# Products of zeros on TensorE in the first stage, and the 32 lag transfers issued by SyncE and GpSimd only

## What is computed

```python
hn = rmsnorm(x, even_norm)
q, k, v, u = split(hn @ even_w_in)             # 256 x (512, 128, 128, 512)
# state-space mixer, for each of 32 groups g of 16 channels, 64 complex states:
dt = exp(log_dt); lam = exp(a * dt)            # a complex, one per state
bb = (lam - 1) / a * b                         # input matrix
h_t = lam * h_(t-1) + bb @ u_t                 # scan over the 256 tokens
y_t = real(c @ h_t) + d_skip * u_t
y = gelu(y); o_ssm = y * sigmoid(y @ w_glu + b_glu)
o_attn = swa_sink_attention(rmsnorm(q), rmsnorm(k), v, sinks)
x = x + concat(o_attn, o_ssm) @ even_w_out
```

## Time and profile before

| | |
|---|---|
| median of 3 runs | 1210.29 us (1207.67 to 1211.19) |
| the profiled execution, its own time | 1210.32 us |
| its span in the trace | 1208.6 us, so 1.7 us lie around it |
| PE busy | 98% |
| PEld, DVE, ACT, POOL busy | 85%, 65%, 49%, 6% |
| mean granted clock of TensorE | 0.997 of full speed |
| chain that ended last | PE 92%, DVE 3%, ACT 2%, DMA 1%, SPq 1% |

### The profile page before, as it was taken

One profiled execution on the slowest core, in us unless ns is written; L12 is line 12 of the kernel. 1 busy time (PEld: TensorE's weight loads), 2 busy tenths in 40 slices (PEclk: granted clock), 3 DMA queues, 4 the chain that ended last, 5 costly groups with the idle time before them and its releaser, 6 DMA issues.

```text
span 1208.6 us, 17835 instructions
## 1 busy us (share of the span) xinstructions
PE 1185.3 (98%) x7139; PEld 1026.1 (85%) x7139; DVE 783.1 (65%) x848; ACT 588.8 (49%) x730; POOL 67.1 (6%) x87
## 2 busy tenths in 40 slices
PE   6999999999999999999999999999999999999997
PEld 5876888888999988888888888888889988888886
DVE  6956676666755557666667666667594646766665
ACT  4547643434566645434345444445574545443443
POOL 2120000000002110000000000000011000000000
PEclk9999999999999999999999999999999999999999
DMA  7254565656544355656555556565543534656561
GB/s 196 92 145 141 162 207 177 200 179 202 180 140 168 113 168 181 207 177 196 185 191 168 199 178 205 177 204 175 175 133 116 183 127 134 197 185 197 179 202 70
DMA packets 156104, 205.81 MB, mean 170 GB/s; under 512 B 7752, under 2 KB 129168, under 8 KB 156048
## 3 DMA queue, kind: packets, MB, share of 16 engines
q1 hardware_dynamic: 154944, 203.30, 52.2%
q10 hardware_dynamic: 944, 1.52, 0.6%
q0 software_dynamic: 160, 0.20, 0.1%
HBM read 202.77 MB, written 1.05 MB: 169 GB/s over the span
## 4 chain that ended last, share of the span: by engine, by line
PE 92%; DVE 3%; ACT 2%; DMA 1%; SPq 1%; issue 0%; POOL 0%; POOLq 0%; ACTq 0%
PE outp L754 26%; PE outp L695 20%; PE acc L695 20%; PE outp L758 14%; PE acc L806 3%; PE outp L713 1%; DMA raw<-in_even_w_in_dram 1%; PE outp L1193 1%; DVE w_lo L2198 1%; PE outp L725 1%; DVE h_pair L2243 1%; PE outp L860 1%; SPq L517 1%; PE acc L1173 1%; ACT w_hi L1650 0%; ACT h_pair L1711 0%
## 5 line engine op out<-in xcount | busy, mean ns | idle before, releaser
L1650 ACT ACTIVATE w_hi<-raw 128x2048 fp32r<-128x2048 f32 x177 | 339.4, 1918 | 413.0 <-PE outp L758 283.2
L2198 DVE TENSOR_TENSOR w_lo<-raw,w_hi 128x2048 fp32r<-128x2048 f32 x177 | 405.3, 2290 | 177.0 <-ACT w_hi L1650 176.9
L754 PE MATMUL outp<-h_pair,w_hi 128*128 128x512 f32 x1056 | 253.9, 391 | 0.3
L754 PEld LDWEIGHTS outp<-h_pair,w_hi 128*128 128x128 f32 x1056 | 195.0, 188 | 42.7 <-DVE h_pair L2243 4.2
L758 PEld LDWEIGHTS outp<-h_pair,w_lo 128*128 128x128 f32 x1056 | 135.4, 191 | 5.2
L695 PE MATMUL acc<-w_hi,f_lo 128*128 128x512 f32 x352 | 137.4, 390 | 0.0
L695 PE MATMUL acc<-w_hi,f_hi 128*128 128x512 f32 x352 | 137.4, 390 | 0.0
L695 PE MATMUL acc<-w_lo,f_hi 128*128 128x512 f32 x352 | 137.1, 389 | 0.0
L758 PE MATMUL outp<-h_pair,w_lo 128*128 128x256 f32 x1056 | 137.0, 283 | 0.0
L695 PE MATMUL outp<-w_hi,h_pair 128*128 128x512 f32 (+1 forms) x416 | 113.9, 361 | 0.3 <-DVE w_lo L2198 0.3
L2297 DVE TENSOR_REDUCE arena<-outp 128x256 f32<-128x512 f32 x88 | 56.7, 686 | 58.4 <-PE outp L758 56.2
(11 more groups left out here) (340 smaller groups left out, 1438.7 us busy)
## 6 DMA issues: line engine op xcount, KB each, us to landing
raw<-in_ffn_w_gate_dram SPq DMA_DIRECT2D x44, 1024.0 KB, 5.6
raw<-in_ffn_w_up_dram SPq DMA_DIRECT2D x44, 1024.0 KB, 5.6
raw<-in_ffn_w_down_dram SPq DMA_DIRECT2D x44, 1024.0 KB, 4.9
raw<-in_odd_w_in_dram SPq DMA_DIRECT2D x12, 1024.0 KB, 5.2
raw<-in_w_in_dram SPq DMA_DIRECT2D x10, 1024.0 KB, 5.2
raw<-in_even_w_in_dram SPq DMA_DIRECT2D x5, 1024.0 KB, 14.4
raw<-in_even_w_out_dram SPq DMA_DIRECT2D x4, 1024.0 KB, 6.8
raw<-in_cross_wk_dram SPq DMA_DIRECT2D x4, 1024.0 KB, 5.7
```

Source lines behind the costliest of these rows:

```text
L754: nc.tensor.matmul(bank, w[0][:, c, m * P:(m + 1) * P], x[:, :, c, :], start=c == 0, stop=c == C - 1, skip_group_check=True)
L1650: A(w_hi[:, slot(u), :], raw[:, u % RAW, :], ACT.Copy).then_inc(w_hi_ready, 1)
L2198: tt(w_lo[:, slot(u), :], raw[:, u % RAW, :], w_hi[:, slot(u), :].bitcast(F32), ALU.subtract).then_inc(w_lo_ready, 1)
```

## The change

Two edits, both in `even`.

**Products of zeros.** DVE sets the first 256 columns of `f_hi` to zero as its first instruction (`zeros_ready`). PE multiplies zeros by zeros (128x128 by 128x256, float32, the shape of L713) at four places: 24 times ahead of the flips of `a_raw`, 12 times ahead of `whole_t(u0)`, 4 times ahead of the wait for `uc`, and 4 times ahead of the wait for `vt`. The results go into banks whose next matmul starts afresh.

**Lag transfers.** SP issues the first 16, POOL the last 16, ACT none.

```diff
+        zeros = f_hi[:, 0:L].bitcast(F32)
...
-        M_SP, M_POOL, M_ACT = m_moves[:15], m_moves[15:20], m_moves[20:]
+        M_SP, M_POOL, M_ACT = m_moves[:16], m_moves[16:], []
...
+            def keep_clock(bank, n):
+
+                for i in range(n):
+                    nc.tensor.matmul(bank[:, 0:L], zeros[:, 0:P], zeros, start=True, stop=True)
+
             def even():
                 u0, k0 = UNITS["even"], OUT["even"] - 2
+                pe.wait_ge(zeros_ready, 1)
+                keep_clock(acc[:, (ACC["norm0"] + 3) % NB, :], 24)
                 pe.wait_ge(consts_in, 16)
...
                 ins.then_inc(bc_flipped, 1)
+                out_taken(pe, OUT["even_u0"])
+                keep_clock(outp[:, OUT["even_u0"] % NB, :], 12)
                 whole_t(u0, OUT["even_u0"], fresh=chunks(0))
...
                 u_chunked(1)
+                out_taken(pe, k0 + 3)
+                keep_clock(outp[:, (k0 + 3) % NB, :], 4)
                 emptied(pe, ACC["uc"], 8)
...
+                keep_clock(outp[:, (k0 + 3) % NB, :], 4)
                 emptied(pe, ACC["u"], 2)
...
                 u0, k0 = UNITS["even"], OUT["even"] - 2
+                V.memset(zeros, 0.0).then_inc(zeros_ready, 1)
                 dve.wait_ge(x_loaded, 16)
```

More of the change, by code:

```diff
@@ L390, in build @@
         stored = sem("stored")
+        zeros_ready = sem("zeros_ready")
         row_flipped, row_ready, half_hi, half_lo = sem("row_flipped"), sem("row_ready"), sem("half_hi"), sem("half_lo")
```

## The result

The changed kernel takes 1213.80 us (median of 9 runs, 1212.80 to 1214.12), the kernel before 1210.05 us (9 runs, 1207.67 to 1211.19). The ratio on record is 1.0038 with a 95% interval of 1.0029 to 1.0047; that of the two medians is 1.0031. So the change makes the kernel 0.3 to 0.4% slower. The profiled execution took 1213.08 us with a span of 1211.3 us, 2.7 us more than before. PE is now busy 99% of the span and the page's chain is PE to 96%, more than in the earlier trace rows: PE waits less, and the kernel ends later.

What follows compares the result with a forecast made beforehand. PE was taken to bound the kernel, so a shift of the first stage's end passes through to the end. Terms of 2.65 - 0.3 + 0.2 = +2.6 us on 1210.3 us gave 1212.9 us, range 1210.0 to 1216.8.

Steps and rivals of the forecast that it cites:

- The 24 products: Ahead of the flips of `a_raw`: start at about 1.3 us, end between 13.7 and 15.0, taken as 14.3.
- B's flips: 32 flips ahead of the 12 products: 0.7 us at full speed, against 1.97 before.
- The 12 products: Ahead of the first projection: 5.3 us at the high level, 17.1 to 22.4, nothing covering them.
- the first term: Head of the kernel: first projection ends at 29.5 instead of 26.85, +2.65 us, bounds +2.0 to +4.6.
- The two waits: Four products at each: +0.68 and +0.74 us beyond the idle time, -1.7 for the kept clock; second term -0.3 us.
- rival C: Clock falls at 50 us all the same: +1.4 in place of -0.3, 1214.6 us; chance 0.14.
- VectorE's room: DVE's chain ahead of its release at 65.11: 3.1 us later, hidden behind 4.0 us of room plus PE's shift.
- The transfers: Lag transfers ahead of `convolve`, SP 16 and POOL 16: third term +0.2 us, from -0.1 to +0.7.
- Rival A: Products at the head are hidden and the clock is won: +0.1 us in all, 1210.4 us; chance 0.07.
- Rival B: POOL's queue of lag transfers becomes the last: +3.4 us in the third term, 1216.1 us; chance 0.09.
- Rival D: Zeros do not raise the clock at the start: +22.4 us, 1232.7 us; chance 0.04.
- The column of the granted clock: At the first projection it shows 1.00 despite half rate; prediction used the rate; by the column the sum is 3.0 us higher.

Runs made afterwards that it cites:

- contig_b: Changed kernel with B's 32 flips reading 128 neighbouring columns instead of every 16th (another B): flips took 1.18 us instead of 1.95, one execution.
- products_only: Changed kernel with all 44 products but the lag transfers as before (SyncE 15, GpSimd 5, ScalarE 12): 1213.42 us, ratio to before 1.0034.
- no_fours: Changed kernel without the 4 and 4 products at the two waits, 24 and 12 kept: 1213.18 us, ratio to before 1.0033.
- no_12: Changed kernel without the 12 products, the 24, 4 and 4 kept: 1210.41 us, ratio to before 1.0019.
- fitted: Changed kernel with 14, 2, 2 and 2 products in place of 24, 12, 4 and 4: 1206.70 us, ratio to before 0.9982.
- lags_only: Changed kernel without any products, the new split of lag transfers kept: 1209.76 us, ratio to before 1.0004.
- double_24: Changed kernel with 48 products at the head in place of 24: span 1222.8 us, one execution.
- fitted_b: `fitted` with two `bst` copies moved from VectorE to ScalarE and 2 more products ahead of PE's wait for B: 1206.56 us, ratio to before 0.9977.

## Why the prediction was right, and where it wasn't

The forecast was 1212.9 us and the range 1210.0 to 1216.8; measured were 1213.80. The likeliest class, within 0.3%, is not where it ended: at +0.38%, with an interval from 0.29 to 0.47 (+0.31% by the medians), it lies just in the class that had 0.36. The sum is to be compared with the profiled executions, +2.6 against +2.76. That it came so near is in part luck: its three terms were off by +0.65, -0.1 and -0.4 us, and the errors cancel.

- **What bounds the kernel.** Right. The shift at `convolve` is the shift at the end, to 0.1 us.
- **The 24 products.** They ended at 13.79, within the bounds 13.7 and 15.0 and 0.5 us before the value taken. The step that failed is the choice of the middle between the two stretches of lower clock: it lasted 3.8 us. Over the runs of the same 24 it ranged from 2.8 us (`contig_b`, 12.06 us against 10.66) to 6.0 us (`products_only`, 13.64), so the range was needed, and the middle was as good as any.
- **B's flips.** The term that was mis-sized: 0.7 us were taken from a row with the same form, 1.95 measured, the same as at the lower clock before. The row at 86.33 is of flips whose source lies in neighbouring columns. The form in the profile (32x32, 32*128) says nothing of the step between the elements that are read; `contig_b` shows 1.18 us without it; the remaining 0.5 us is open (the row at 86.33 also takes turns over four blocks of partitions, not two). The upper bound, 1.97, held.
- **The 12 products.** 5.38 us, predicted 5.3, nothing covering them. With the two errors above (-0.5 and +1.25, which partly cancel) and a projection of 6.91 us in the chain where 7.1 was taken, the first term came out at +3.3 instead of +2.65, within its bounds of 2.0 to 4.6.
- **The two waits.** Both idle times are gone, the clock stays at 1.00, and the term is 2.91 - 3.30 = -0.4, predicted -0.3. `no_fours` confirms the fall without them (rival C's ground) and that the four and four pay 0.5 us.
- **VectorE's room.** Predicted to hide 3.1 us behind 4.0 us of room. Its chain ended 2.7 us later (67.95 - 4.13 = 63.82 against 61.11) and was hidden; the release moved with PE, from 65.11 to 67.95. `no_12` and `fitted` show the wait that appears once PE is quicker.
- **The transfers.** Predicted +0.2, measured -0.2 (2.71 - 2.91). Of that 0.1 us is the wait of before, 79.46 to 79.57, which is gone; the rest is PE's own. The prediction had the two meet again at 82, and they do: `convolve` starts at 82.28 right behind PE's flips, and only the loading of its weights had waited 0.2 us for the last landing. SP's longest issue is 604 ns here, not 898 (with ScalarE silent too, single ones took 1005 ns in `lags_only` and 1612 in `double_24`), and POOL's pitch is (78.5 - 71.0) / 15 = 0.50 us. The last landing came 11.5 us after SP's first issue, before 11.6. The Trainium skill ("DMA: Bandwidth & Descriptors", section "Issuing engines are not separate DMA queues") says that all issuers share the same 16 DMA engines and that spreading saves only the time of issuing. The measured ratio of 1.0004 for the new split agrees, as far as its interval (0.9994 to 1.0013) tells.
- **Rival A** (hidden products) did not come, but `fitted` is what it would have looked like with a smaller number. **Rival B** (POOL's queue): POOL's longest issue was 769 ns again, its median 484, though DVE worked beside them, and POOL did not decide. **Rival D**: refuted by the rate from 5 us on.
- **The gap to the threshold.** The median moved 1.0 us more than the profiled executions. The prediction took the profiled execution of before for its median; runs of the same program spread over 3.7 us, in part through the clock, so that a sum made on one execution has an error of about 1 us that no row of it shows. This belongs into the range, and into the chances: here it decided on which side of 0.3% the time came to lie.
- **The column of the granted clock.** It was right to go by the rates. After, the column is 1.00 while the first products run at half rate, as before at the first projection, and in `lags_only` it is 1.00 while 16 flips take 3.68 us at 9.70, where 2.03 is their time at full clock. These flips ran at the lower level before too; the prediction's "twice" leaves them out, without harm to the sum, since PE waited for the weight behind them. But the caveat in the Trainium skill that the prediction cites, that recorded clock events have been seen to be unreliable, is not borne out by this case. (That page asks for the throttled time to be compared with a model of its cost; the comparison with single durations is the prediction's own.) The entries of the packed traces fit the rates: 22.75 us before and 5.15 after for the rise, 17.1 to 20.5 in `lags_only` for the fall. What misled is the column, which prints 1.00 ahead of the first entry.

## What to carry to other kernels

Work that only keeps an engine awake is free up to the idle time that it fills and counts in full beyond that, so it is sized by that idle time and by its own duration at the lower clock: 20 products gave -0.2%, 44 gave +0.4%. Before filling a wait, look what the same engine's next real work releases elsewhere: holding up a flip of 0.3 us by 4 us moved the end of VectorE's chain by 2.7 us, and as soon as PE was quicker (`no_12`) that chain was the bound. And where two events meet within 0.1 us, as PE and the transfers at 79.5 us, a gain in one of them is capped by the other, and by the third that comes next.

## What was not expected of the hardware

- 32 transposes with a source step of 64 bytes took 1.97 us at the lower level (before) and 1.95 at the upper (after), and 1.18 us there with neighbouring columns (`contig_b`): the clock does not set their time, and the step sets 0.8 us of it.
- PE's rate doubles at another time in each execution, with the same work issued before: the trace's entry for it stands at 22.75 us in the kernel before and at 13.71 in `lags_only`, where PE had run nothing but flips since 9.38. The 16 matmuls of the first projection took 10.14 us in the one and, with the fall behind it, 8.86 in the other.
- Products of zeros raised the clock like the matmuls of real data, within 2.8 to 6.0 us of starting at 1.25 us (24 products); in the first projection of before it took 6.1 us.
- The clock fell to 0.5 behind 32 short transposes with 0.63 us of idle time ahead of them (`fitted_b`), and did not with 0.20 us (`fitted`).
